# mLSTM heads: gate and convolution projections between the attention's steps, a head's normalisation and gating beside the next head's projections

## The reference

```python
q, k, v, o, g, gb, gc, u = jnp.split(h @ w_in, splits, axis=-1)
# per head and direction (forward, backward), log weights from the gates g
d = jnp.exp(log_d - m[..., None])
s = jnp.einsum('bhcjd,bhcsd->bhcjs', q, k) * d
num = jnp.einsum('bhcjs,bhcsv->bhcjv', s, v) + ...
h = num / jnp.maximum(jnp.abs(den), jnp.exp(-m))[..., None]
...
hn = rms_norm(h.transpose(0, 2, 1, 3), mnorm_g.reshape(ML_HEADS, ML_DV))
og = jax.nn.sigmoid(o)
m_out = hn * og
c_out = gb * short_conv(gc * u, conv_w)          # three taps along the tokens
y = jnp.concatenate([m_out, c_out], axis=-1) @ w_out
```

## Time and profile before

| | |
|---|---|
| median of 3 runs | 4517.87 us (4515.65 to 4518.29) |
| the profiled execution | 4513.81 us, its span 4512.0 us |
| TensorE, VectorE, ScalarE, GpSimd busy | 90%, 47%, 33%, 36% of the span |
| the four heads | about 114 to 732 us |
| start of each head's first tile | 114.20, 274.42, 431.95, 589.43 us |

### The profile page before, as it was taken

The page is one execution under the profiler, slowest core; times in us unless marked ns, Lnnn a source line. Parts: engine busy times, 40 slices in busy tenths (PEclk is TensorE's granted clock), DMA queues, the critical chain, the costliest instruction groups (busy, mean ns, idle before and its releaser), DMA issues.

```text
span 4512.0 us, 63014 instructions
## 1 busy us (share of the span) xinstructions
PE 4050.0 (90%) x20662; PEld 3358.9 (74%) x20662; DVE 2130.2 (47%) x3452; ACT 1486.3 (33%) x2395; POOL 1644.2 (36%) x2044
## 2 busy tenths in 40 slices
PE   4688688899997988999999999989988999998997
PEld 3577578899996776788777678768866776876885
DVE  5445544522334776333564642443357366235225
ACT  3111111211123654222454543222236365333223
POOL 0011012333332112566424335446632433544564
PEclk7688789899998999999999999989989999998998
DMA  3133121111111000222212112222221211322222
GB/s 136 47 141 117 55 105 52 47 61 61 60 61 39 23 24 31 89 96 95 85 43 75 49 64 94 84 75 93 97 64 47 75 52 52 99 80 69 94 97 84
DMA packets 92780, 328.61 MB, mean 73 GB/s; under 512 B 10240, under 2 KB 12544, under 8 KB 92544
## 3 DMA queue, kind: packets, MB, share of 16 engines
q1 hardware_dynamic: 90928, 323.61, 21.6%
q10 hardware_dynamic: 1616, 1.90, 0.1%
HBM read 323.38 MB, written 2.10 MB: 72 GB/s over the span
## 4 chain that ended last, share of the span: by engine, by line
issue 67%; POOL 32%; POOLq 1%
POOL Wl L264 32%; POOLq L259 0%; POOLq L261 0%; POOLq L264 0%; POOLq L147 0%; POOLq L258 0%; POOLq L3209 0%
## 5 line engine op out<-in xcount | busy, mean ns | idle before, releaser
L264 POOL TENSOR_TENSOR Wl<-raw,Wh 128x256 fp32r<-128x256 f32 x2040 | 1644.0, 836 | 2867.3 <-ACT Wh L357 2867.2
L357 ACT ACTIVATE Wh<-raw 128x1024 fp32r<-128x1024 f32 x510 | 540.2, 1059 | 1941.3 <-PE psum L1063 1696.6
L1061 PE MATMUL psum<-Hh,Wh 128*128 128x512 f32 (+1 forms) x2704 | 1045.7, 387 | 79.3 <-DVEq L1892 60.9
L1062 PE MATMUL psum<-Hl,Wh 128*128 128x512 f32 (+1 forms) x2704 | 1019.1, 377 | 0.0
L1063 PE MATMUL psum<-Hh,Wl 128*128 128x512 f32 (+1 forms) x2704 | 1018.7, 377 | 0.0
L1061 PE MATMUL psum<-Gh,Wh 128*128 128x512 f32 (+3 forms) x2032 | 753.0, 371 | 27.1 <-DVEq L1892 23.3
L1063 PE MATMUL psum<-Gh,Wl 128*128 128x512 f32 (+3 forms) x2032 | 745.1, 367 | 0.0
L1062 PE MATMUL psum<-Gl,Wh 128*128 128x512 f32 (+3 forms) x2032 | 745.0, 367 | 0.0
L1061 PEld LDWEIGHTS psum<-Hh,Wh 128*128 128x128 f32 x2704 | 519.4, 192 | 212.9 <-DVEq L1892 67.0
L1063 PEld LDWEIGHTS psum<-Hh,Wl 128*128 128x128 f32 x2704 | 519.5, 192 | 72.6
L1062 PEld LDWEIGHTS psum<-Hl,Wh 128*128 128x128 f32 x2704 | 520.8, 193 | 66.9 <-issue 2.5
(11 more groups left out here) (331 smaller groups left out, 4813.7 us busy)
## 6 DMA issues: line engine op xcount, KB each, us to landing
raw<-in_wstream SPq DMA_DIRECT2D x510, 512.0 KB, 3.3
stage<-in_ada SPq DMA_DIRECT2D x80, 512.0 KB, 4.2
M<-in_ada SPq DMA_DIRECT2D x16, 512.0 KB, 4.9
X<-in_xT SPq DMA_DIRECT2D x1, 2048.0 KB, 12.0
out<-X SPq DMA_DIRECT2D x8, 256.0 KB, 2.0
X<-in_ctxT SPq DMA_DIRECT2D x1, 1024.0 KB, 7.1
M<-in_memT ACTq DMA_DIRECT2D x1, 1024.0 KB, 6.6
M<-in_axial ACTq DMA_DIRECT2D x1, 512.0 KB, 3.6
```

The source lines that it names most:

```text
L264: last = pool.tensor_tensor(Wl[:, s, c], raw[:, s, c], Wh[:, s, c].bitcast(F32), ALU.subtract)
L357: act.activation(Wh[:, s], raw[:, s], ACT.Copy).then_inc(v["w_high"], 1)
L1061: pe.matmul(dst, a[0], b[0], start=first, stop=False)
L1062: pe.matmul(dst, a[0], b[1], start=False, stop=False)
```

## The change

The eight tiles of step (4) are called fills 0 to 7 here (`projected`). Five of them stand between the steps of the attention (`ML_BESIDE`: after steps 0 and 2 of group 0, after steps 1, 3 and 5 of group 1), three behind the groups (`ML_BEHIND`: one, then two). Each keeps its ada products. ScalarE copies gate, gc and gb out of PSUM into parts of `M`, VectorE multiplies u onto gc there. After every second fill ScalarE converts the next weight block. The convolution follows a head's last division; its root, normalisation, gating and the splits into `Gh`, `Gl` stand between VectorE's work on the next head's query, key and value tiles. Before `w_out`, the first block is multiplied in parts, so that it waits last for head 3's rows. The gate rows move to other partitions (`gate_rows`), and the split probabilities signal TensorE through `hand_free` instead of a semaphore instruction of their own.

```diff
+ML_BESIDE, ML_BEHIND = {0: (0, 2), 1: (1, 3, 5)}, {0: 1, 1: 2}
+ML_GIVEN = 1 + 2 * 8 + 1 + 4
...
+        def projected(h, i):
+            nonlocal point
+            kind, j = i // 2, i % 2
+            c = slice(j * HALF, (j + 1) * HALF)
+            b = tiles.look(act)
+            if kind != 2:
+                kept = (gate_raw, cu, None, last_raw)[kind]
+                act.activation(kept[:, c], psum[:, b, 0:HALF], ACT.Copy).then_inc(v["bank_free"][b], 1)
+            tiles.skip(ada_tiles(point))
+            point += 1
+            if j == 1:
+                next_weights()
...
+                    if step in ML_BESIDE[group]:
+                        projected(h, fill)
+                        fill += 1
                 act.wait_ge(for_act, wants.next())
                 for j in range(2):
                     give(psum[:, 6 + j, 0:n], ACT.Abs, n)
                 tiles.skip(2)
+                for _ in range(ML_BEHIND[group]):
+                    projected(h, fill)
+                    fill += 1
             for _ in range(2):
                 from_bank(tiles.look(act), HALF, ACT.Sqrt, scale=1.0 / ML_DV, bias=sc[:, 60:61])
-            for _ in range(2):
-                from_bank(tiles.look(act), HALF, ACT.Sigmoid)
-                tiles.skip(ada_tiles(point))
-                point += 1
-            next_weights()
-            for _ in range(3):
-                point = used_beside_ada(2, point)
+            for j in range(2):
+                give(gate_raw[:, j * HALF:(j + 1) * HALF], ACT.Sigmoid, HALF)
...
+            def projected():
+                nonlocal w, fill, point
+                if fill % 2 == 0:
+                    w = weights()
+                project(w, slice(0, P), H, *ALL_SEGS[fill % 2])
+                ada(point)
+                fill += 1
+                point += 1
...
-                    wait_ready()
+                    if not started:
+                        pe.wait_ge(v["acc_free"], acc.next())
+                    pe.wait_ge(v["hand_free"], weighed.next())
...
+                    if step in ML_BESIDE[group]:
+                        projected()
                 for d in range(2):
-                    exact(P, n, v["selh"][0:4, :], M[0:4, (2 + d) * TOK + g0:(2 + d) * TOK + g0 + n])
+                    exact(P, n, v["selh"][64 + 32 * d:68 + 32 * d, :], gate_rows(v, d)[1][:, g0:g0 + n])
+                weighed.next(2)
+                for _ in range(ML_BEHIND[group]):
+                    projected()
+            weighed.next(4)
             wait_ready()
             for j in range(2):
                 exact(P, HALF, ones, tab[:, 1280 + j * HALF:1280 + (j + 1) * HALF])
-            for _ in range(4):
-                w = weights()
-                for t0, n in ALL_SEGS:
-                    project(w, slice(0, P), H, t0, n)
-                    ada(point)
-                    point += 1
-        wait_ready()
-        for m in range(KT):
+        w = weights()
+        banks = [tiles.take(pe) for _ in ALL_SEGS]
+        for ks in ((0, 1, 2, 4, 5, 6), (7,), (3,)):
+            if len(ks) == 1:
+                wait_ready()
+            for b, (t0, n) in zip(banks, ALL_SEGS):
+                for k in ks:
+                    mm = mm3(psum[:, b, 0:n], (w[0][:, k, :], w[1][:, k, :]), (Gh[:, k, t0:t0 + n], Gl[:, k, t0:t0 + n]), k == 0, k == 3)
+                if k == 3:
+                    mm.then_inc(v["tile_done"], 1)
+        for m in range(1, KT):
...
-        def probabilities(n=SEQ, lo=0, hi=SEQ, times=None):
+        def probabilities(lo, hi, times):
             dve.wait_ge(v["acc_done"], pv.next())
             s = p_slot[0] % 2
             p_slot[0] += 1
             e = take(SEQ)[:, lo:hi]
-            if times is not None:
-                tt(e, times, e, ALU.mult)
-            split(Ph[:, s, lo:hi], Pl[:, s, lo:hi], e)
-            give_back()
-            for_pe()
+            tt(e, times, e, ALU.mult)
+            cp(Ph[:, s, lo:hi], e)
+            dve.tensor_tensor(Pl[:, s, lo:hi], e, Ph[:, s, lo:hi].bitcast(F32), ALU.subtract).then_inc(v["hand_free"], 1)
...
+        def projected(h, i):
+            nonlocal point
+            kind, j = i // 2, i % 2
+            if kind == 2:
+                b = look()
+                tt_last(b, cu[:, halves[j]], psum[:, b, 0:HALF], cu[:, halves[j]], ALU.mult)
+            else:
+                tiles.skip(1)
+            ada(point)
+            point += 1
+        def convolve(h):
+            w = [vec[:, VEC["conv_w"] + 4 * i + h:VEC["conv_w"] + 4 * i + h + 1] for i in range(3)]
+            for p0, pn, _ in PARTS:
+                p1 = p0 + pn
+                ts(y[:, p0:p1], cu[:, p0:p1], w[1], ALU.mult)
+                stt(y[:, p0 + 1:p1], cu[:, p0:p1 - 1], w[0], y[:, p0 + 1:p1], ALU.mult, ALU.add)
+                stt(y[:, p0:p1 - 1], cu[:, p0 + 1:p1], w[2], y[:, p0:p1 - 1], ALU.mult, ALU.add)
+        def normed(h):
+            for j in range(2):
+                stt(h32[:, halves[j]], h32[:, halves[j]], vec[:, VEC["mg"] + h:VEC["mg"] + h + 1], roots[j], ALU.mult, ALU.mult)
+        def gated(h):
+            for j in range(2):
+                tt(h32[:, halves[j]], h32[:, halves[j]], take(HALF), ALU.mult)
+                give_back()
+            split(Gh[:, h, :], Gl[:, h, :], h32)
+        def convolved(h):
+            tt(y, last_raw, y, ALU.mult)
+            split(Gh[:, 4 + h, :], Gl[:, 4 + h, :], y)
...
+                if h > 0:
+                    (normed, gated)[j](h - 1)
             values(look(), 0, 4, P)
             ada(point)
+            if h > 0:
+                convolved(h - 1)
...
+                steps = ML_KEYS[group]
...
+                masked(0)
+                for step, (kt, dirs) in enumerate(steps):
                     b = look()
                     for d in dirs:
                         lo, hi, _ = ml_range(group, kt, d)
-                        probabilities(lo=lo, hi=hi, times=psum[:, b, lo:hi])
+                        probabilities(lo, hi, psum[:, b, lo:hi])
                     free(b)
+                    if step + 1 < len(steps):
+                        masked(step + 1)
+                    if step in ML_BESIDE[group]:
+                        projected(h, fill)
+                        fill += 1
...
+                if group == 1:
+                    tt(sq, h32, h32, ALU.mult)
+                    for_pe()
+                for _ in range(ML_BEHIND[group]):
+                    projected(h, fill)
+                    fill += 1
+            convolve(h)
             for j in range(2):
-                bank_rstd((S0, S1)[j][:, 0:HALF], HALF)
...
+                bank_rstd(roots[j], HALF)
+        convolved(3)
+        for_pe()
+        normed(3)
+        gated(3)
```

More of the change, by code:

```diff
@@ L301, in ml_range, with hybrid_scratch, gate_rows @@
     return (P * j, n, P * j) if d == "f" else (0, P * (j + 1), P * j)
+def hybrid_scratch(v):
+    M = v["M"]
+    return [M[:, i * TOK:(i + 1) * TOK] for i in (1, 2, 3)] + [M[:, 3328:4096]]
+def gate_rows(v, d):
+    M = v["M"]
+    return M[32 * d:32 * d + 4, 0:TOK], M[64 + 32 * d:68 + 32 * d, 0:TOK]
 def latent_scratch(v):
@@ L495, in _ @@
             point = used_beside_ada(2, point)
+            fill = 0
             for group, n in ((0, CTX), (1, SEQ)):
                 tiles.skip(2)
-                for kt, dirs in ML_KEYS[group]:
+                for step, (kt, dirs) in enumerate(ML_KEYS[group]):
                     act.wait_ge(for_act, wants.next())
@@ L1237, in _ @@
         pe.wait_ge(v["rows_done"], 2)
-        point = 0
+        point, weighed = 0, Count(2 + ML_GIVEN)
         for h in range(ML_HEADS):
@@ L1273, in _ @@
                 left = {d: sum(d in dirs for _, dirs in steps) for d in "fb"}
-                for kt, dirs in steps + ((None, ""),):
+                for step, (kt, dirs) in enumerate(steps + ((None, ""),)):
                     if kt is not None:
@@ L2230, in _ @@
                 dve.sem_inc(v["acc_free"], 1)
-            tt(sq, h32, h32, ALU.mult)
-            for_pe()
-            for j in range(2):
-                bank_rstd((S0, S1)[j][:, 0:HALF], HALF)
-            for j in range(2):
-                hj = h32[:, j * HALF:(j + 1) * HALF]
-                stt(hj, hj, vec[:, VEC["mg"] + h:VEC["mg"] + h + 1], (S0, S1)[j][:, 0:HALF], ALU.mult, ALU.mult)
-                b = look()
-                tt(hj, hj, take(HALF), ALU.mult)
-                give_back()
-                free(b)
-                ada(point)
-                point += 1
@@ L2244, in _ @@
-            split(Gh[:, h, :], Gl[:, h, :], h32)
-            cu, y = tab[:, 0:TOK + 4], tab[:, TOK + 4:2 * TOK + 4]
-            for j in range(2):
-                b = look()
-                cp((S0, S1)[j][:, 0:HALF], psum[:, b, 0:HALF])
-                free(b)
-                ada(point)
-                point += 1
-            for c in (0, CTX + 1, CTX + 2, TOK + 3):
-                do(dve.memset(cu[:, c:c + 1], 0.0))
-            for j, (t0_, n) in enumerate(ALL_SEGS):
```

(29 more changed lines are left out.)

49 lines of the change are left out of this document (28 added, 21 removed).

## The result

The changed kernel takes 4471.46 us (median of 4 runs, 4468.70 to 4474.29), the kernel before beside it 4516.76 (4513.37 to 4518.29): a ratio of 0.9905, 95% interval [0.9894, 0.9916], 45.3 us less. The forecast was 56 less and 4462, with a range of 4420 to 4502. The profiled execution took 4468.70 us, its span 4465.8.

A forecast was written before the change was run, and what follows sets the result against it. Attention was taken as a VectorE-ScalarE-TensorE chain leaving TensorE waiting at low clock. Heads 0 to 2 -38, head 3 -28, GpSimd conflict +10: -56 us, giving 4458 profiled, 4462 median, range 4420 to 4502.

The forecast's parts named there:

- (a): Heads 0 to 2, attention entry to the first division: 21.0 us would become 30.6, +9.6 a head.
- (b): Heads 0 to 2, division of group 0 to first probabilities of group 1: one more ada pair on VectorE, +1.0.
- (c): Heads 0 to 2, group 1, probabilities of key block 0 to those of block 2: 11.9 us becomes 21.0, +9.1.
- (d): Heads 0 to 2, group 1, key block 2 to the division: 24.4 us becomes 29.9, +5.5.
- (e): Heads 0 to 2, second division to the next dense tile, over fills 6 and 7: 14.2 us becomes 15.0, +0.8.
- (f): After heads 0 to 2, the next head's query/key and value tiles up to its entry: 31.5 us before, +8.4.
- Heads 0 to 2: Projection stretch between heads removed, -47.2 us, with +34.4 coming back: -12.8 a head, -38 for three.
- Head 3: Last head, no ada blocks left: attention unchanged, tail to the second output tile shorter; -28 us.
- The lock of GpSimd and VectorE: GpSimd subtractions after conversions slow VectorE's chain, 0.8 us for three of four conversions in four heads: +10 us.
- The gating itself ... hides under the value tiles: Next head's projections: about 5 us of VectorE gating hidden under 17 us of value tiles; otherwise costs those 5.
- second rival: Low TensorE clock continues through the next head's projections: 4613 us at worst, 4566 if half comes; chance 0.08.
- The weight wait: Heads 0 to 2: 12 waits of 6.2 us for weight blocks; rival that they fall away: 4385 us, chance 0.08.

The follow-up runs named there:

- experiment 11: The changed kernel run once more, unaltered: 4478.95 us in one run, the kernel before beside it 4509.15.
- experiment 5: The changed kernel with no fills between the attention's steps, four behind each group instead: 4476.93 us, ratio 0.9919 to the kernel before.
- experiment 1: The changed kernel with SyncE issuing each weight block before the ada blocks of its turn: 4380.49 us, ratio 0.9700 to the kernel before.
- experiment 2: The changed kernel with ScalarE's weight conversions moved behind work the chain waits for, SyncE's order unchanged: 4385.24 us, ratio 0.9717 to the kernel before.
- experiment 10: The kernel before with constants two columns wider, moving every later tensor by 8 bytes: 4515.66 us, ratio 0.9997 to the kernel before.

## Why the prediction was right, and where it was off

The mechanism of the sum held in each place. The steps of head 0, forecast and measured (from the rows above, each from one step's start to the next): (a) 30.6 and 30.0; (b) 10.0 and 9.7; (c) 21.0 and 20.1; (d) 29.9 and 31.2; (e) 15.0 and 15.7; (f) 39.9 and 41.4. The head: 146.3 and 148.1. That each step agrees within 1.5 us is in part luck: in experiment 11 the same three heads took 149.6, 146.8 and 153.0. One term was misread as well: the backward values of key block 1 were done 16.8 us after the entry in the kernel before (163.6), not 16, so (a) should have been 31.4.

**Heads 0 to 2.** From entry to entry 148.1, 149.1 and 147.9 us, before 159.1, 157.8 and 157.2: 11.0, 8.7 and 9.3 less, 29 together where "-12.8 each" gave 38. Two terms were a little small, (f) by 1.5 and (d) by 1.3, and I had used head 0 for all three, though heads 1 and 2 were 1.3 and 1.9 us shorter before.

**Head 3.** -28 forecast, 28.0 less measured, from its entry to the first blocks of `w_out`, and both parts hold. The attention to the end of its division took 72.0 us, before 71.3 (I had put it at 0). The tail behind it, the kernel before first:

```profile
692.18:740.72 48.54, 46.54 (x250) 45.01 (x251) 20.76 (x33) 7.56 (x10) 13.83 (x16) 0.94 0.14 44
```

```profile
665.27:685.02 19.75, 13.60 (x53) 11.56 (x54) 16.17 (x20) 3.49 (x5) 1.31 (x2) 0.76 0.10 28
```

28.8 less. One sign to look for did not show: the waits inside `w_out` were 3.54 and 2.50, not the 8 to 10 that I wanted to see.

**The lock of GpSimd and VectorE.** +10 was too much. The cast and the subtraction at 208.71 and 209.54, beside three GpSimd subtractions, took 0.79 and 1.09 where the same pair took 0.43 and 0.69 alone at 188.65: 0.76 more. But only one conversion in a head had such operations of the chain beside it; the reciprocals of the divisions took 1.75 and 3.35 as without it. About 2 us in three heads, and they are in the measured heads already. So two errors of the sum cancel, by luck: the heads gave 9 less than forecast, and the 10 for the lock was not to be paid beside them. At the first blocks of `w_out` the changed kernel was 55.7 us ahead (29.1 and 28.0, less 1.4 by which its first entry came later), and the forecast was 56. The Trainium skill, "SBUF — State Buffer", section "SBUF: two separate sides", has the lock last for one whole instruction; GpSimd's subtractions take about 0.7 us each (2.78 for four at 177.97), so the 0.36 and 0.40 more at 208.71 and 209.54 don't contradict it. What no row shows is my reading of it, all 2.8 us of a conversion.

**The fills' places.** "Fill 0 runs where TensorE stood: free" and its like were right as steps, but experiment 5 shows that the places between the steps, taken together, were worth 5.5 us here, by the traces most of it in head 3. The rest of the gain is in what both orders have: fills under the two divisions, and a shorter tail of head 3. How it splits between those in heads 0 to 2 wasn't tried.

**"The gating itself ... hides under the value tiles ...; without that cover it would cost those 5."** This place of the forecast failed. The 5 were right as a wait (5.10) and wrong as a price: 24 a head. This is the second rival's mechanism, the low clock going on through the next head's projections. In the changed kernel TensorE also waits (6.12 + 0.95 us before 268.81), but a query and key tile of 384 columns stands behind, and the clock is back before the value tiles. I had priced that rival from the first projections alone, which also begin with such a tile; none of my rows showed what value tiles do behind a wait.

**The weight wait.** Its rival ("does not bite") was wrong, and its price there, 4385, looks exact: experiments 1 and 2 took it away and measured 4380 and 4385. But I had priced the waits at 77 us (4462 less 4385), and they were worth 86 to 91; the kernel that they were taken from was itself 9 us above the forecast. The landing took 5.3 to 5.8 us, not 6.2.

**What was not forecast.** Of the 55.7 us, 9.4 went back behind the heads, in code that the change does not touch; hence 45.3 and not 56. One place shows how: the same seven weight blocks, before and after.

```profile
1304.70:1366.00 61.30, 58.45 (x337) 58.13 (x336) 21.23 (x38) 14.15 (x21) 22.23 (x28) 1.00 0.18 61
```

```profile
1247.60:1311.80 64.20, 61.34 (x338) 61.03 (x337) 21.31 (x38) 14.20 (x21) 22.30 (x29) 0.95 0.18 58
```

2.9 us more for the same work, and a granted clock of 0.95 instead of 1.00. Such places are scattered over the rest of the program. They are not the whole of it: from the first blocks of `w_out` to the end TensorE was busy for 3508.4 us, in the kernel before for 3504.0, so only 4.4 of the 9.4 are longer busy time and 5.0 are idle. The traces' clock has it low for 296 us there, in the kernel before for 288, and in experiment 10, which gave back 1.0, for 300: more low clock alone does not make a kernel give back. Experiment 10 rules out the tensors' places. Experiment 11 speaks against an accident of one execution: 13.4 us went back there. The kernels made from the changed one gave back 6 to 14 us, experiment 1 too (9.5), those made from the kernel before at most 1. Why the changed heads have this effect behind them stays open.

The best kernel is that of experiment 1: 4380 us, 3.0% under the kernel before.

## What to carry to other kernels

When work is moved between the steps of a chain, move it with everything that its engines must do for it: here a conversion that waits for a DMA came along and stood in front of the exponentials, and one line in SyncE's order was worth twice as much as the whole change. Read the wait of a helper engine by what is queued behind it, not by its sum: nearly the same sum (215 us before, 218 after) cost 19 before and 91 after. And price a new TensorE wait by what runs behind it as well, with the durations at both clock levels.

## What the hardware showed that I had not expected

After a wait of 5.1 us TensorE stayed at 1.2 GHz for 47.8 us (the profile's clock, 276.8 to 324.6): through 39.2 us without idle, nearly all of it products of 128 columns (417 ns each, 277 at 2.4 GHz), and on into the next attention. In another order, after 6.12 and 0.95 us of wait, it was back at 2.4 GHz inside one tile of 384-column products. With 24 such products put in front (5.2 us) the value tiles ran at 2.4 GHz, and the program was 39 us shorter for doing more. The Trainium skill, "TensorE: Matmul & The Clock Gate", section "Part 1: The HAM clock gate", speaks of a clock that comes back under sustained work; the rows of the value tiles don't agree with that as it stands.
